# Sums of weight blocks by accumulating DMAs in a seven-product MLP down projection

## The reference

```
h2 = rms_norm(x, ln_mlp_pre)
ff = jnp.square(jax.nn.relu(h2 @ w_up)) @ w_down
return x + rms_norm(ff, ln_mlp_post)
```

## Time and profile before

| what | value |
|---|---|
| median of 3 runs | 1913.14 us (1912.83 to 1913.59) |
| the profiled execution | 1912.04 us, of which the span is 1910.1 us |
| PE busy | 1851.4 us (97%) |
| DVE busy | 1322.6 us (69%) |
| ACT busy | 754.2 us (39%) |
| POOL busy | 205.4 us (11%) |
| DMA | 190.01 MB, 99 GB/s over the span |

### The profile page before, as it was taken

How to read it: one execution, slowest core, us unless ns; L and a number is a source line. 1 busy time by engine, 2 the same in 40 slices (tenths; PEclk the granted TensorE clock), 3 DMA queues, 4 the chain that set the end, 5 groups by cost and what they waited for, 6 DMA issues and landing times.

```text
span 1910.1 us, 23505 instructions
## 1 busy us (share of the span) xinstructions
PE 1851.4 (97%) x8622; PEld 1489.4 (78%) x8622; DVE 1322.6 (69%) x2128; ACT 754.2 (39%) x1259; POOL 205.4 (11%) x317
## 2 busy tenths in 40 slices
PE   8999999999999999999799999999999999999996
PEld 6877767888888787878578767678888887878784
DVE  6865889753475768586868658887434768585768
ACT  3163352421335544435431533524122355445353
POOL 2221111011220000000012211111112100000000
PEclk9999999999999999999999999999999999999998
DMA  6432213322521231414222322232225222314031
GB/s 243 138 117 82 68 65 97 83 67 78 220 100 53 104 113 64 152 58 144 81 87 94 133 71 68 67 97 72 78 78 220 89 75 81 136 51 165 34 111 44
DMA packets 73218, 190.01 MB, mean 99 GB/s; under 512 B 18384, under 2 KB 30864, under 8 KB 72080
## 3 DMA queue, kind: packets, MB, share of 16 engines
q1 hardware_dynamic: 43200, 159.31, 24.2%
q10 hardware_dynamic: 29904, 29.19, 4.6%
HBM read 177.42 MB, written 11.06 MB: 99 GB/s over the span
## 4 chain that ended last, share of the span: by engine, by line
PE 87%; DVE 6%; issue 4%; ACT 3%; DMA 0%; DVEq 0%; ACTq 0%; SPq 0%
PE psD L1167 22%; PE psD L1169 22%; PE psD L1168 22%; PE psM L1167 3%; PE psM L1169 3%; PE psM L1168 3%; PE psM L1226 2%; DVE d_lo L2459 1%; PE psM L1240 1%; PE psM L1435 1%; PE psM L1233 1%; PE psM L1453 1%; PE psM L1332 1%; PE psM L1441 1%; DVE wide L2469 1%
## 5 line engine op out<-in xcount | busy, mean ns | idle before, releaser
L1167 PE MATMUL psD<-a_hi,w_hi 128*128 128x512 f32 (+2 forms) x1488 | 594.7, 400 | 0.9 <-DVE w_lo L1054 0.6
L1169 PE MATMUL psD<-a_hi,w_lo 128*128 128x512 f32 (+2 forms) x1488 | 575.9, 387 | 0.0
L1168 PE MATMUL psD<-a_lo,w_hi 128*128 128x512 f32 (+2 forms) x1488 | 574.8, 386 | 0.0
L1054 DVE TENSOR_TENSOR w_lo<-raw,w_hi 128x1024 fp32r<-128x1024 f32 x216 | 264.4, 1225 | 134.0 <-POOL w_hi L1153 96.5
L1167 PEld LDWEIGHTS psD<-a_hi,w_hi 128*128 128x128 f32 (+1 forms) x1488 | 279.3, 188 | 75.6 <-issue 21.3
L1169 PEld LDWEIGHTS psD<-a_hi,w_lo 128*128 128x128 f32 (+1 forms) x1488 | 279.0, 187 | 57.8
L1168 PEld LDWEIGHTS psD<-a_lo,w_hi 128*128 128x128 f32 (+1 forms) x1488 | 279.6, 188 | 56.9 <-issue 4.3
L1152 POOL TENSOR_TENSOR w_hi<-raw,tabs 128x1 fp32r<-128x1 f32 x152 | 35.0, 230 | 1278.2 <-PE psD L1169 1247.1
L1153 POOL TENSOR_SCALAR w_hi<-raw 128x1023 fp32r<-128x1023 f32 x152 | 169.4, 1115 | 0.0
L2459 DVE TENSOR_TENSOR d_lo<-d_raw,d_hi 128x1024 fp32r<-128x1024 f32 x104 | 125.9, 1222 | 60.0 <-ACT d_hi L1984 60.0
L1984 ACT CAST d_hi<-d_raw 128x1024 fp32r<-128x1024 f32 x104 | 108.0, 1047 | 128.9 <-DVE d_raw L2436 82.9
(11 more groups left out here) (285 smaller groups left out, 2918.4 us busy)
## 6 DMA issues: line engine op xcount, KB each, us to landing
raw<-in_ws SPq DMA_DIRECT2D x216, 512.0 KB, 3.4
d_raw<-in_wd SPq DMA_DIRECT2D x64, 512.0 KB, 4.5
s_raw<-in_wo ACTq DMA_DIRECT2D x14, 512.0 KB, 11.4
tabs<-in_tab SPq DMA_DIRECT2D x2, 2944.0 KB, 12.3
x<-rows_d ACTq DMA_DIRECT2D x4, 1024.0 KB, 5.8
x<-out ACTq DMA_DIRECT2D x2, 2048.0 KB, 8.2
x<-in_x SPq DMA_DIRECT2D x4, 512.0 KB, 5.9
out<-x SPq DMA_DIRECT2D x4, 512.0 KB, 8.2
```

What stands on the lines that cost most here:

```text
L1054: dve.tensor_tensor(w_lo[:, s, :], raw[:, s, :], w_hi[:, s, :].bitcast(F32), ALU.subtract) \
L1167: pe.matmul(out, lhi, rhi, start=start, stop=False, skip_group_check=more)
L1168: pe.matmul(out, lhi, rlo, start=False, stop=False, skip_group_check=more)
L1169: return pe.matmul(out, llo, rhi, start=False, stop=stop, skip_group_check=more)
```

## The change

- The sums of weights are no longer made by DVE. d_raw has nine places (HOMES). SP loads a first block into each (FIRST_IN), POOL adds further blocks from HBM by DMAs that accumulate into the place (add), and a product reads the place when the right number of adds has landed (SUMMED, landed_at). A place goes through several sums: C0 holds b12, then b12+b11 for P5, then also b22 for P6, then also b21 for P4.
- Only additions are left there, so signs move: S1 becomes A22 - A21, S2 and S4 are formed with a factor of -1 (combine, combine2), and evictions into the second half of the columns subtract (evict).
- In a chunk SP loads nine first blocks and two reloads (A0 and A1 with b12, once P1's remainders are made); the next chunk's first blocks are loaded in the order of FREED, each behind the split that reads its place last, all at the chunk's last weight slab in SP's queue. POOL issues nine adds a chunk in a written order with waits between them.
- STEPS has P5's first half as second step. combine2 stands ahead of the next slab's ahead. Evictions of P1 and P2 come one step later (AFTER).
- The first two slabs of the next layer are rounded by ACT (round_up), not by POOL.

```diff
-STEPS = [("P1", 0), ("P2", 0), ("P1", 1), ("P2", 1), ("P5", 0), ("P5", 1), ("P6", 0), ("P6", 1), ("P3", 0), ("P3", 1),
+STEPS = [("P1", 0), ("P5", 0), ("P2", 0), ("P1", 1), ("P2", 1), ("P5", 1), ("P6", 0), ("P6", 1), ("P3", 0), ("P3", 1),
          ("P7", 0), ("P7", 1), ("P4", 0), ("P4", 1)]
+HOMES = ("A0", "C0", "B0", "A1", "C1", "E", "B1", "D0", "D1")
+FREED = {"B0": ("P2", 0), "B1": ("P2", 1), "C1": ("P5", 1), "D0": ("P3", 0), "D1": ("P3", 1), "A0": ("P7", 0), "A1": ("P7", 1),
+         "C0": ("P4", 0), "E": ("P4", 1)}
+SUMMED = {("P5", 0): ("sum_C0", 1), ("P5", 1): ("sum_C1", 1), ("P6", 0): ("sum_C0", 2), ("P6", 1): ("sum_E", 2),
+          ("P7", 0): ("sum_A", 1), ("P7", 1): ("sum_A", 2), ("P4", 0): ("sum_C0", 3), ("P4", 1): ("sum_E", 3)}
...
+                        if m >= SL_MLP and (m - SL_MLP) % CT == CT - 1:
+                            c = (m - SL_MLP) // CT
+                            for j in range(2):
+                                sp.wait_ge(*on(*split_at(c, "P1", j)))
+                                sp.dma_start(home(f"A{j}"), down_slab(c, "b12", j)).then_inc(*inc("d_in3", 16))
+                            for name, step in FREED.items() if c < CHUNKS - 1 else ():
+                                sp.wait_ge(*on(*split_at(c, *step)))
+                                sp.dma_start(home(name), down_slab(c + 1, *FIRST_IN[name])).then_inc(*inc(BATCH[name], 16))
...
-                    if layer < DEPTH - 1:
-                        for m in range(2):
-                            pool.wait_ge(*on("w_hi", NSLAB + m))
-                            round_(layer * NSLAB + NSLAB + m)
+                    def add(c, name, b, j):
+                        pool.dma_start(home(name), down_slab(c, b, j), accum_op=ALU.add).then_inc(*inc("sum_" + name[:None if name[0] == "C" else 1], 16))
+
+                    for c in range(CHUNKS):
+                        pool.wait_ge(*on("d_in0", 16 * BATCHES["d_in0"] * (c + 1)))
+                        add(c, "C0", "b11", 0)
+                        pool.wait_ge(*on("d_in1", 16 * BATCHES["d_in1"] * (c + 1)))
+                        add(c, "E", "b12", 1)
+                        add(c, "C1", "b11", 1)
+                        pool.wait_ge(*on("sum_E", 16 * (3 * c + 1)))
+                        add(c, "E", "b22", 1)
+                        pool.wait_ge(*on("sum_C0", 16 * (3 * c + 1)))
+                        pool.wait_ge(*on(*split_at(c, "P5", 0)))
+                        add(c, "C0", "b22", 0)
+                        pool.wait_ge(*on("d_in3", 16 * BATCHES["d_in3"] * (c + 1)))
+                        add(c, "A0", "b22", 0)
+                        pool.wait_ge(*on("sum_A", 16 * (2 * c + 1)))
+                        add(c, "A1", "b22", 1)
+                        pool.wait_ge(*on("sum_C0", 16 * (3 * c + 2)))
+                        pool.wait_ge(*on(*split_at(c, "P6", 0)))
+                        add(c, "C0", "b21", 0)
+                        pool.wait_ge(*on("sum_E", 16 * (3 * c + 2)))
+                        pool.wait_ge(*on(*split_at(c, "P6", 1)))
+                        add(c, "E", "b21", 1)
...
+                    def combine2(c, p):
+
+                        dve.wait_ge(*on("comb", 4 * (c * PAIRS + p) + 1))
+                        sig(dve.scalar_tensor_tensor(out=fr[:, S2, :], in0=fr[:, S3, :], scalar=-1.0, in1=fr[:, A22, :],
+                                                     op0=ALU.mult, op1=ALU.subtract), "comb")
...
-                    AFTER = {2: "P1", 3: "P2", 5: "P5", 7: "P6", 9: "P3", 11: "P7", 13: "P4"}
-                    THEN = {1: (t2, 0), 2: (t2, 1), 4: (t3, 0), 6: (t3, 1), 8: (t4, 0), 9: (t4, 1)}
+                    AFTER = {3: "P1", 4: "P2", 5: "P5", 7: "P6", 9: "P3", 11: "P7", 13: "P4"}
...
-                    for t, args in ((t3, 1), (t4, 0), (t4, 1)):
-                        t(c, args)
```

More of the change, by code:

```diff
@@ L84 @@
 DOWN_SLOT = {("b11", 0): 0, ("b21", 0): 1, ("b11", 1): 2, ("b21", 1): 3, ("b12", 0): 4, ("b12", 1): 5, ("b22", 0): 6, ("b22", 1): 7}
-WITH = [("A", 4)] * 4 + [("B", 2)] * 2 + [("C", 2)] * 2
-MADE = {("P5", 0): 1, ("P5", 1): 2, ("P6", 0): 3, ("P6", 1): 4, ("P7", 0): 5, ("P7", 1): 6, ("P4", 0): 7, ("P4", 1): 8}
+HOMES = ("A0", "C0", "B0", "A1", "C1", "E", "B1", "D0", "D1")
+FIRST_IN = {"A0": ("b11", 0), "C0": ("b12", 0), "B0": ("b21", 0), "A1": ("b11", 1), "C1": ("b12", 1), "E": ("b11", 1),
+            "B1": ("b21", 1), "D0": ("b22", 0), "D1": ("b22", 1)}
+BATCH = {"A0": "d_in0", "C0": "d_in0", "B0": "d_in0", "A1": "d_in1", "C1": "d_in1", "E": "d_in1", "B1": "d_in1", "D0": "d_in2", "D1": "d_in2"}
+BATCHES = {"d_in0": 3, "d_in1": 4, "d_in2": 2, "d_in3": 2}
+FREED = {"B0": ("P2", 0), "B1": ("P2", 1), "C1": ("P5", 1), "D0": ("P3", 0), "D1": ("P3", 1), "A0": ("P7", 0), "A1": ("P7", 1),
+         "C0": ("P4", 0), "E": ("P4", 1)}
+SOURCE = {("P1", 0): "A0", ("P1", 1): "A1", ("P2", 0): "B0", ("P2", 1): "B1", ("P3", 0): "D0", ("P3", 1): "D1",
+          ("P5", 0): "C0", ("P5", 1): "C1", ("P6", 0): "C0", ("P6", 1): "E", ("P7", 0): "A0", ("P7", 1): "A1",
+          ("P4", 0): "C0", ("P4", 1): "E"}
+SUMMED = {("P5", 0): ("sum_C0", 1), ("P5", 1): ("sum_C1", 1), ("P6", 0): ("sum_C0", 2), ("P6", 1): ("sum_E", 2),
+          ("P7", 0): ("sum_A", 1), ("P7", 1): ("sum_A", 2), ("P4", 0): ("sum_C0", 3), ("P4", 1): ("sum_E", 3)}
+SUMS = {"sum_C0": 3, "sum_C1": 1, "sum_E": 3, "sum_A": 2}
 DOWN = [("down", [c * CT + 4 * j + (b[1] == "2") + 2 * i for i in range(2)], 2, (b[2] == "2") * S, S)
@@ L756, in build @@
             d_lo = sb("d_lo", [P, RING, SLAB], F32R, where=mlp)
-            d_raw = sb("d_raw", [P, len(DOWN_SLOT), SLAB], where=mlp)
+            d_raw = sb("d_raw", [P, len(HOMES), SLAB], where=mlp)
         psD = [ctx.enter_context(nc.psum_tensor(f"psD{i}", [P, S], F32)) for i in range(4)]
@@ L892, in operand, with home, down_slab, landed_at @@
             return d_hi[:, r, :], d_lo[:, r, :]
+        def home(name):
+            return d_raw[:, HOMES.index(name), :]
         def source(st):
[L895 to L901, removed]
+            return home(SOURCE[STEPS[st]])
+        def down_slab(c, b, j):
+            return wd[layer * len(DOWN) + c * CT + DOWN_SLOT[b, j]]
+        def landed_at(c, q, j):
+            if (q, j) in SUMMED:
+                name, n = SUMMED[q, j]
+                return name, 16 * (SUMS[name] * c + n)
+            batch = BATCH[SOURCE[q, j]]
+            return batch, 16 * BATCHES[batch] * (c + 1)
+        def split_at(c, q, j):
+            return "d_lo", c * NSTEP + STEPS.index((q, j)) + 1
         def operand_free(eng, c, st):
@@ L1132, in _ @@
                             sp.wait_ge(*on("d_lo", 0))
-                            sp.wait_ge(*on("T", 0))
                             sp.dma_start(tabs2[:], tab[:, basics:]).then_inc(kept["tables_in"], 16)
[L1135 to L1144, removed]
+                        if m == SL_MLP:
+                            sp.wait_ge(*on("slab_done", SLAB_OF["out0", 0] + 1))
+                        if SL_MLP <= m < SL_MLP + CT:
+                            for name in HOMES[m - SL_MLP:m - SL_MLP + (1 if m < SL_MLP + CT - 1 else 2)]:
+                                sp.dma_start(home(name), down_slab(0, *FIRST_IN[name])).then_inc(*inc(BATCH[name], 16))
+                        if m >= SL_MLP and (m - SL_MLP) % CT == CT - 1:
[6 more added lines that the diff above has]
+                                sp.dma_start(home(name), down_slab(c + 1, *FIRST_IN[name])).then_inc(*inc(BATCH[name], 16))
                 @block.gpsimd
@@ L1566, in product @@
                         q, j = STEPS[st]
-                        a, _, bank = PRODUCTS[q]
+                        a, bank = PRODUCTS[q]
                         hi, lo = operand(c, st)
@@ L1961, in round_up @@
                         n = SL_MLP + c * CT + i + 2
-                        if n < NSLAB:
+                        if layer * NSLAB + n < DEPTH * NSLAB:
                             s = (layer * NSLAB + n) % 2
@@ L2418, in _, with combine @@
                     lo_x1(READY)
[L2420 to L2448, removed]
+                    def combine(c, p):
+                        dve.wait_ge(*on("f_sq", c * CT + 2 * p + 2))
+                        sig(dve.tensor_tensor(fr[:, S3, :], fr[:, A11, :], fr[:, A21, :], ALU.subtract), "comb")
+                        sig(dve.tensor_tensor(fr[:, S1, :], fr[:, A22, :], fr[:, A21, :], ALU.subtract), "comb")
+                    def combine2(c, p):
+                        dve.wait_ge(*on("comb", 4 * (c * PAIRS + p) + 1))
+                        sig(dve.scalar_tensor_tensor(out=fr[:, S2, :], in0=fr[:, S3, :], scalar=-1.0, in1=fr[:, A22, :],
+                                                     op0=ALU.mult, op1=ALU.subtract), "comb")
+                        dve.wait_ge(*on("comb", 4 * (c * PAIRS + p) + 3))
+                        sig(dve.scalar_tensor_tensor(out=fr[:, S4, :], in0=fr[:, A12, :], scalar=-1.0, in1=fr[:, S2, :],
```

(19 more changed lines are left out.)

16 lines of the change are left out of this document (3 added, 13 removed).

## The result

The changed kernel takes **1896.08 us** (median of 4 runs, 1894.17 to 1899.82); the kernel before took 1912.99 us beside it. The ratio is 0.9915, with an interval of 0.9897 to 0.9932: 16.9 us faster. The forecast was 35.5 us, a time of 1877.6. The sign and the range held, the size did not: just under half of the forecast gain came.

What follows compares the result with a forecast made beforehand. TensorE was held to wait in the down product for VectorE's remainders; 20.2 + 10.1 + 8.0 - 2.8 = 35.5 us off 1912.0 gave 1876.5, on the median's scale 1877.6 us. Own range 1871 to 1884, upper end 1900.

Steps and rivals of the forecast that it cites:

- the lateness of the last sums: In chunk 3, A1's sum lands 1.4 us late at each layer's end: -2.8 us in the forecast.
- X = 6: Time of one accumulating DMA, issue to landing, taken as 6 us from the row of a 1024 KB transfer (5.8 us).
- T0: Start of a chunk's down product, its first matmul; the prediction counts its times in the chunk from there.
- The middling rival: Adds of 7.5 to 9.5 us, since 20 DMAs a chunk share the engines: 1886 to 1899 us, chance 0.13.
- Slow adds: Software-filled queue makes A1's sum late; gain eaten at 9.9 us an add, 1938 us at 11.4; chance 0.14.
- The subtractions' price: All 64 weight subtractions leave DVE, 78.1 us; gains 20.2 us in chunks 0 to 2, 10.1 and 8.0 in chunk 3.
- Six phases without late sums: Down phases of chunks 0 to 2, both layers: 21.4 us lost before, 0.2 us a chunk kept, gain 20.2 us.
- L: Start of the first tile's eviction in chunk 3, forecast at T0+21.4; moving it moves the layer's end.
- The two ends without lateness: Chunk 3's chain to the layer's end comes earlier by 10.1 us in layer 0 and 8.0 in layer 1.
- POOL against DVE: Rival: POOL's issuing slows DVE, 0.74 us each time, on chunk 3's chain: 1884 us, chance 0.07.
- "Issue" as PE's own: Rival: PE's 13.7 us of waits named issue are its own and stay: 1891 us, chance 0.05.
- SP's late weight load: Up slab i=2's load, behind the next chunk's loads, goes out at T0+32.9, with 6 us of cover.

Runs made afterwards that it cites:

- number 5: Changed kernel with the add into A0 issued after its own reload, and chunk 0's blocks loaded three at a time: 1874.66 us.
- number 2: Changed kernel with SP's first loads for the next chunk cut to 16 of 1024 columns, adds whole: 1879.17 us.
- number 4: Kernel before the change, with VectorE's 64 subtractions of weight blocks on 16 of 1024 columns: 1878.69 us.
- numbers 1: Changed kernel with POOL's adds moving 16 of 1024 columns, as many issues as before: 1874.9 us.
- numbers 3: Changed kernel with separate counts for A0's and A1's reloads, so A0's add goes out after its own reload: 1879.19 us.

## Why the prediction was right or wrong

**What failed: the lateness of the last sums, -2.8 us in the sum, measured at about -23** (17.2 in the six phases, 2.4 and 3.2 at the ends, against number 5). Three things in that step were wrong.

- *X = 6.* The size came from a row of plain loads that were issued two at a time, and "they are busy 0.12 in the down phases" was put against the middling adds. That was the share before the change; the change itself raises it to 0.66 to 0.93. Alone an add takes 5.2 to 5.5 us, so the guess was good for a lone one. Beside the next chunk's loads A0's add took 8.3 to 9.7 us in chunks 1 and 2, and in number 2, without them, 5.4 to 5.5.
- *"C0 about 1 us after" A1.* Two adds that go out together share the engines: C0 landed 2.7 and 3.8 us after A1 in chunk 3, and 3.8 to 5.0 in chunks 0 to 2. At the ends this was the step that failed: a lone add took less than 6 us there, but the square of tile 0 had to wait for C0 and began 2.6 us behind the T0+23.85 of the prediction, in layer 0.
- *No deadline for E.* For chunks 0 to 2 the prediction priced A1 alone, wanted by T0+27.5. A1 landed at 26.3 to 28.0 in five of the six phases, so that price was right and nearly nothing. But the sum behind it in the queue, E's, was wanted by 33.0 and landed at 35.0 to 37.5. The prediction names it as "issued behind that" and leaves it without a deadline, so its lateness stood in the sum at nothing, without a reason. In five of the six phases it is the one that decided, 11.9 of the 17.2 us; the other 5.3 are A1's, in layer 1's chunk 1.

**The middling rival** had the right mechanism and, by luck more than by its working, about the right time: at X of 8 to 9 it gave 1886 to 1899. Its price was placed on A1; it fell on E, and at the ends on C0. **Slow adds** did not come: A0's add took up to 9.7 us, but A1's only 5.5 to 7.5 in five of the six phases, so the price of 12 us a us on A1 was due in the sixth only (10.1).

**What was right.** The subtractions' price: number 4 gives 34.4 us. Six phases without late sums: 229.3 us in numbers 1, 2 and 5, forecast 229.7. L: T0+21.57 against 21.4 in layer 0. A0's add at T0+11.3 to 11.5 against 11.0, though in chunk 0 of both layers at 13.4. The two ends without lateness, in number 5: 9.9 us in layer 0 (forecast 10.1), and 50.5 us from T0 to the end of layer 1, 8.0 us less than before, as forecast. The forecast without its lateness is 38.3 us; number 5 has 37.8.

**POOL against DVE:** refuted. Two adds are issued from 915.20 on, for 1.79 us; the d_lo that DVE starts at 915.91 takes 1.22 us, as ever, and none of the 104 d_lo of the run takes more than 1.23. The four combinations take 0.42 us each, the scalar-tensor-tensor kind too. For the rounding the contention was real; issuing does not have it. The Trainium skill, SBUF — State Buffer, Who interferes with whom, speaks of GpSimd instructions that read SBUF; for the issue of a DMA these rows show no such contention.

**"Issue" as PE's own:** refuted. In number 4, where only the subtractions shrink, PE has no gap in the six phases (its busy time is their length), and none without late sums either.

**SP's late weight load:** forecast at T0+32.9, hidden. In chunk 1 it goes out at 767.02, T0+37.9, because E's split is late, and PE's waits for w_lo are 0.6 us in all: still hidden.

The Trainium skill, DMA: Bandwidth & Descriptors, Anatomy of one DMA, gave an estimated 3.2 us for an add. The plain copies agree with it (3.4 us at the least); the adds do not (5.2 us at the least).

**Two slips without effect.** 21.4 us in six phases are 3.6 us a chunk, not 3.5. And the two combinations that took 1.62 us beside the rounding answer to the pair at 646.85, which took 0.76 us, not to the later pair of 0.88: the slowing was 0.86 us.

**Left open.** Why layer 1's chunk 1 is worse than the others: its A1 and C0 took 10.1 and 13.3 us, and no run isolates that; in numbers 3 and 5 too A1's add is slowest in this phase (9.9 and 10.1 us). The mixing part of layer 1 took 1.2 us more than before (631.1 against 629.9); its cause was not sought.

## What to carry to other kernels

When work moves from an engine to DMAs, the DMA share of before is no evidence: add the change's own transfers to it, stage by stage, and take X from a row with that load beside it. In a queue of dependent transfers, write down a deadline for each, the last above all; here, in five of six phases, every us of E's landing past T0+33.0 cost a us. Before making transfers faster, look at what starts the chain: one semaphore shared by two reloads cost 17 us.

## What the hardware showed beyond that

- An accumulating DMA of 512 KB takes 5.2 to 5.5 us alone where a copy takes 3.5, and keeps the 16 DMA engines busy for 2.9 us instead of 1.5.
- With a ring of 1024 B a partition two of these DMAs are in flight and the third issue waits on POOL, shown as "issue"; with 512 B one (+48 us), with 1536 B three, at no gain. Of plain copies three go out in a row with 1024 B.
- Issuing one takes POOL about 0.87 us (a copy 0.53), and no slowing of DVE shows beside it.
